# DVE's order beside the convolutions of a hybrid decoder layer: taps first, the weight remainder in two halves around the other work

## What is computed

```python
xn = rmsnorm(h, norm1_w[layer])
proj = xn @ w_in[layer]
q, k, v, z, xbc, dt_raw, ga_raw, gs_raw = _split(proj, IN_SPLITS)
attn = banded_sink_attention(q, k, v, attn_sinks[layer]) @ w_attn_o[layer]
xbc = jax.nn.silu(causal_dwconv(xbc, ssd_conv_w[layer], ssd_conv_b[layer]))
xs, bm, cm = _split(xbc, (D_INNER, BC_DIM, BC_DIM))
y = ssd_chunked(xs.reshape(Bsz, S, N_SSD_HEADS, SSD_HEAD_DIM), dt, a_log[layer], ...)
```

## The kernel before

| stage | DVE: unit, slot | PE: needs it at unit, slot |
|---|---|---|
| probabilities 5 | (9, 0) slot 0 | (9, 1) slot 0, L1321 |
| probs_t_masked 5 | (9, 1) slot 0 | (10, 0) slot 0, L1331 |
| probabilities 7 | (10, 1) slot 1 | (11, 0) slot 1, L1321 |
| probabilities 9 | (12, 1) slot 0 | (13, 0) slot 0, L1321 |
| probabilities 14 | (16, 0) slot 0 | (16, 1) slot 0, L1321 |
| decayed_cb 8 | (31, 0) slot 0 | (31, 1) slot 0, L1363 |

## Time and profile before

### The profile page before, as it was taken

How to read it: one execution, slowest core, us unless ns; L and a number is a source line. 1 busy time by engine, 2 the same in 40 slices (tenths; PEclk the granted TensorE clock), 3 DMA queues, 4 the chain that set the end, 5 groups by cost and what they waited for, 6 DMA issues and landing times.

```text
span 1028.8 us, 13393 instructions
## 1 busy us (share of the span) xinstructions
PE 1019.6 (99%) x5095; PEld 832.2 (81%) x5095; DVE 642.0 (62%) x909; ACT 457.5 (44%) x818; POOL 69.4 (7%) x112
## 2 busy tenths in 40 slices
PE   9999999999999999999999999999999999999997
PEld 8887777777788888888888888898888888888886
DVE  7636999794476685985754544666666676641323
ACT  6344555454555545765533222544444444331233
POOL 0000000000231120122220100000000000000000
PEclk9999999999999999999999999999999999999999
DMA  7622221225556424445362743223232223332322
GB/s 219 123 85 82 83 62 63 83 83 120 159 133 162 133 72 137 140 127 153 100 205 82 266 143 108 77 82 113 91 122 82 82 85 119 93 128 87 95 69 82
DMA packets 123498, 116.48 MB, mean 113 GB/s; under 512 B 21342, under 2 KB 111782, under 8 KB 123447
## 3 DMA queue, kind: packets, MB, share of 16 engines
q1 hardware_dynamic: 95509, 94.74, 29.9%
q10 hardware_dynamic: 25346, 12.59, 5.2%
q0 software_dynamic: 2592, 8.46, 2.2%
HBM read 109.41 MB, written 6.36 MB: 113 GB/s over the span
## 4 chain that ended last, share of the span: by engine, by line
PE 89%; DVE 8%; ACT 2%; issue 1%; DMA 0%; SPq 0%; ACTq 0%; DVEq 0%
PE banks L1259 27%; PE banks L1260 27%; PE banks L1261 27%; DVE conv_acc L1207 3%; PE banks L1363 1%; DVE w_lo L856 1%; PE banks L1356 1%; PE banks L1331 1%; PE banks L1351 1%; PE banks L1339 1%; DMA w_raw<-in_w_in 0%; ACT probs L614 0%; PE banks L1321 0%; PE banks L1311 0%; ACT w_hi L576 0%
## 5 line engine op out<-in xcount | busy, mean ns | idle before, releaser
L856 DVE TENSOR_TENSOR w_lo<-w_raw,w_hi 128x1024 fp32r<-128x1024 f32 (+1 forms) x166 | 198.3, 1234 | 123.7 <-ACT w_hi L576 122.4
L576 ACT ACTIVATE w_hi<-w_raw 128x1024 fp32r<-128x1024 f32 (+1 forms) x166 | 164.1, 1037 | 109.2 <-PE banks L1261 107.9
L1259 PE MATMUL banks<-xn_hi,w_hi 128*128 128x512 f32 x528 | 211.5, 401 | 0.0
L1260 PE MATMUL banks<-xn_lo,w_hi 128*128 128x512 f32 x528 | 206.1, 390 | 0.0
L1261 PE MATMUL banks<-xn_hi,w_lo 128*128 128x512 f32 x528 | 206.0, 390 | 0.0
L1259 PE MATMUL banks<-hn_hi,w_hi 128*128 128x512 f32 (+1 forms) x376 | 141.3, 376 | 0.0
L1260 PE MATMUL banks<-hn_lo,w_hi 128*128 128x512 f32 (+1 forms) x376 | 141.2, 375 | 0.0
L1261 PE MATMUL banks<-hn_hi,w_lo 128*128 128x512 f32 (+1 forms) x376 | 141.2, 375 | 0.0
L1259 PEld LDWEIGHTS banks<-xn_hi,w_hi 128*128 128x128 f32 x528 | 99.1, 188 | 28.2 <-issue 8.5
L1261 PEld LDWEIGHTS banks<-xn_hi,w_lo 128*128 128x128 f32 x528 | 99.1, 188 | 21.4
L1260 PEld LDWEIGHTS banks<-xn_lo,w_hi 128*128 128x128 f32 x528 | 99.3, 188 | 19.0
(11 more groups left out here) (221 smaller groups left out, 1429.8 us busy)
## 6 DMA issues: line engine op xcount, KB each, us to landing
w_raw<-in_w_in SPq DMA_DIRECT2D x29, 1024.0 KB, 5.4
w_raw<-in_w_up SPq DMA_DIRECT2D x22, 1024.0 KB, 5.0
decay<-acs_scratch ACTq DMA_DIRECT2D x16, 512.0 KB, 5.9
w_raw<-in_w_ssd_o SPq DMA_DIRECT2D x8, 1024.0 KB, 5.3
w_raw<-in_w_down SPq DMA_DIRECT2D x8, 1024.0 KB, 5.0
w_raw<-in_w_in SPq DMA_DIRECT2D x16, 256.0 KB, 4.5
w_raw<-in_w_attn_o SPq DMA_DIRECT2D x16, 256.0 KB, 4.7
decay_off<-acs_scratch ACTq DMA_DIRECT2D x32, 128.0 KB, 3.6
```

The costliest lines, as they stand in the source:

```text
L576: A.activation(whi[:, c % 2, lo_:hi_], raw[:, c % 2, lo_:hi_], ACT.Copy).then_inc(w_rounded, 1)
L856: V.tensor_tensor(wlo[:, c % 2, lo_:hi_], raw[:, c % 2, lo_:hi_], f32(whi[:, c % 2, lo_:hi_]), ALU.subtract).then_inc(w_split, 1)
L1259: T.matmul(out_, w[0], m[0], start=first, stop=False)
L1260: T.matmul(out_, w[0], m[1], start=False, stop=False)
```

## The change

In a chunk with a convolution, DVE no longer starts with the whole `split(c + 1)` and the rides of slot 0. For unit 0 its order is now: three taps, first half of `split(c + 1)`, rides of slots 0 and 1, second half, end of the silu (L1212, now L1218), rides of slot 2. For unit 1: three taps, rides of slots 0 and 1, end of the silu, rides of slot 2. In all other chunks nothing moves. No instruction is added or removed; only DVE's order differs.

```diff
-            def split(c, pairs=0):
+            def split(c, pairs=0, part=(0, 1)):
 
-                for k, (lo_, hi_) in enumerate(halves(c)):
+                for k in part:
+                    lo_, hi_ = halves(c)[k]
                     eng.wait_ge(w_rounded, 4 * pairs + (2 * c + k + 1))
...
-                elif 1 < c + 1 < len(CHUNKS) and c not in (AT[("out", 3)], AT[("up", 0)]):
+                elif 1 < c + 1 < len(CHUNKS) and c not in (AT[("out", 3)], AT[("up", 0)]) and kind not in ("bc", "xs"):
                     split(c + 1)
...
                 for u in range(2):
-                    rides(c, u, 0)
                     if kind not in ("bc", "xs"):
+                        rides(c, u, 0)
                         rides(c, u, 1)
...
+                        if u == 0:
+                            split(c + 1, part=(0,))
+                        rides(c, u, 0)
                         rides(c, u, 1)
+                        if u == 0:
+                            split(c + 1, part=(1,))
                         eng.wait_ge(c_tanh, k_conv + 1)
```

## The result

| | before | changed |
|---|---|---|
| median of the runs beside each other | 1030.29 us (1030.12 to 1030.65, 4 runs) | 1055.55 us (1054.08 to 1056.15, 4 runs) |
| ratio to before, 95% interval | 1 | 1.0243 (1.0225 to 1.026) |
| profiled execution, own time | 1030.5 us | 1054.08 us |
| its span | 1028.8 us | 1052.3 us |
| mean granted clock of PE in it | 0.999 | 0.992 |

Slower by 25.3 us, where 17.1 were forecast; the time lies above the range's 1054.

A forecast was written before the change was run, and what follows sets the result against it. PE, busy 1019.6 of 1028.8 us, was taken as the bound, so each new wait costs in full. Seven terms sum to 17.1 us on 1030.5, giving 1047.6, or 1047.4 for the median; range 1039 to 1054.

The forecast's parts named there:

- the clock: Rival: PE's clock falls at the two long waits, losing 1.65 us each, 3.3 in all: 1050.7 us; chance 0.15.
- Mechanism: DVE's taps wait for ACT's L772, so rides come late by 2.24 us, plus 1.13 for unit 0's half split.
- seven terms: PE's added waits at places from unit (9, 0) to chunks 31 to 33, 17.1 us in sum.
- term 7: Chunks 31 to 33: PE waits 2.5 us more for decayed_cb and 0.85 more for `x_dt`.
- Terms 1 to 6: Chunks 9 to 28: PE waits for late rides, lastly a late split: 3.95, 1.75, 1.3, 3.5, 2.2, 1.1 us.
- Covered at nothing (chunks 7 and 8): Probabilities and split still come over 1 us early in chunks 7 and 8, so no cost there.
- Signs in the profile: About 4 us PE idle before L1321, named releasers, DVE's idle before taps rising to some 15 us.
- the second rival: Lags don't add up over the long chains of steps; only 10.4 us are lost: 1040.7 us; chance 0.12.
- the third: Rival: faster by 2 us, as banks and tanh are free earlier and rides still make it: 1028.3 us; chance 0.03.
- No effect: Rival: DVE lags so far that L772 is always done before the taps: 1030.3 us; chance 0.04.

The follow-up runs named there:

- experiment 4: Changed kernel plus 16, 16 and 8 matmuls on constants in PE's waits for probabilities 5, 9 and 14: 1049.82 us.
- experiment 6: Kernel before with the new order in chunk 9 alone, plus 16 matmuls on constants in PE's wait for probabilities 5: 1035.7 us.
- experiment 5: Kernel before with the new order in chunk 9 alone, without filling matmuls: 1037.82 us.
- experiment 2: Changed kernel with the whole split back at the chunk's head, so only the rides of slot 0 moved behind the taps: 1043.47 us.
- experiment 1: Changed kernel with the rides of slot 0 back ahead of the taps, only the split's two halves staying behind them: 1041.09 us.
- experiment 3: Changed kernel plus 28, 28 and 14 matmuls on constants in PE's waits for probabilities 5, 9 and 14: 1053.76 us.
- experiment 7: Kernel before with only the split's second half moved behind the rides of slot 1 in convolution chunks: 1030.97 us, ratio 1.0005.

## Why the prediction was right or wrong

The step that failed is the clock, which the sum set at nothing after the long waits. The prediction had it as a rival with a chance of 0.15 and 3.3 us, and spoke against it that the waits "are hardly longer than the 3.3 us of that row, and it is one row". Experiments 4 and 6 show it as a cause: with PE busy in the waits, and nothing else changed, 5.6 and some 2 us went away. The rival's price was too small as well, though its upper bound of 6.6 held the measured 5.62. I counted two falls of 1.65; there were three, of 1.62, 2.41 and 1.59. The second lasted longer, some 6.8 us at the low level (182.4 to 189.2) where the first lasted 3.4. Transposes and scores stood behind both waits, so they don't tell the two apart. What differs in the rows is when the clock fell: 0.1 us after the first wait's end, but 1.7 us before the second's, and 1.1 before it in experiment 5, where it also stayed low for 6.8. What sets that moment no run here shows. The third fall I had not counted, since a wait of 2.1 is shorter than the 3.3 of my one row. The Trainium skill, "TensorE: Matmul & The Clock Gate", section "Why this matters for your kernels", which I had weighed and set aside, was right on the two long waits.

The other steps:

- **Mechanism: right.** The rides come late by the taps and the half split behind a wait for ACT's L772. All seven terms appeared at the place and with the releaser named. The largest loss of PE that no term named is 0.36 us at 465.36, for the second half of a split; the measured term 7 includes it.
- **Terms 1 to 6: right** within 0.15 us each. Laying out each engine's rows by hand with start-to-start prices held over a dozen steps.
- **Term 7: decayed_cb right (2.52), x_dt 10 undersized,** 1.58 for 0.85. Most of this is one DVE row that took 1.22 where it took 0.69 before; its rows are in the last section.
- **Covered at nothing (chunks 7 and 8): right.** Between the start-up and 123.7, PE waits for no ride and no split.
- **Signs in the profile: places right, DVE's idle wrong.** 29.0 us stood before the taps, for "some 15": I had counted idle time only in the units that hand something over late.
- **Rivals.** The lags do add up (18.16 against 17.1), so the second rival falls. Of the gain of the third there is no trace in the changed kernel, since no wait of PE was one for a bank. "No effect" falls with the first row on L1208.

What stays open: the other three timed runs of the changed kernel took 1055.3 to 1056.15 with a mean clock of 0.991, against 1054.08 and 0.992 for the profiled one. More or longer falls of the clock would fit, as in the two pairs of experiment 5; those runs have no trace, so this is argued. The lags and the clock give 17.1 + 1.1 + 5.6 = 23.8, and where the last 1.5 of the median's 25.3 went is not shown.

## What to carry to other kernels

Where one engine is the bound at 99%, an order that makes a helper engine wait first and serve later costs the whole delay, once for every result that had less slack than the delay; a piece of independent work (here one half of the split) must stay in front to fill the wait. Price a long wait of PE as the wait plus the slow matmuls behind it, 1.6 to 2.6 us here, and consider that a wait of 1.9 us can bring them too. Small waits left in a tuned order aren't simply to be had: removing two of them by hand gained 0.9 us in a trace and nothing that the timing could tell, and removing a third brought two others that took it back.

## What was not expected of the hardware

**A clock that falls well after a short wait.** The wait of 2.09 us ended at 239.45, and matmuls ran at full rate until they stretched, in the changed kernel's timeline of PE:

```profile
240.18 0.39 PE L1266 MATMUL banks<-xn_lo,w_hi 128*128 128x512 f32 x1
240.40 0.59 PE L1267 MATMUL banks<-xn_hi,w_lo 128*128 128x512 f32 x1
...
243.35 0.63 PE L1265 MATMUL banks<-xn_hi,w_hi 128*128 128x512 f32 x1
243.78 0.43 PE L1266 MATMUL banks<-xn_lo,w_hi 128*128 128x512 f32 x1
```

Starts are 0.43 us apart instead of 0.23, for 3.4 us, at half the clock and in the midst of dense work. The wait of 2.45 us at 443.08 brought nothing of the kind, nor did those of 1.5 to 1.7. In experiment 2 a wait of 1.88 us was followed by a fall and one of 2.20 us was not. So the length of a wait alone doesn't tell whether the clock falls.

**A DVE operation that stood behind one of POOL.** In the changed kernel around unit (32, 1), DVE and then POOL:

```profile
465.22 1.22 DVE L1218 SCALAR_TENSOR_TENSOR xs<-conv_tanh,conv_acc 128x512 f32<-128x512 f32 x1
...
464.91 0.98 POOL L558 TENSOR_TENSOR y_sq_pair<-y_off 128x256 f32<-128x256 f32 x1 [12.96 <-ACT y_off L672]
```

The same DVE operation takes 0.68 us everywhere else, and POOL's takes 0.74 where they don't meet, as in the kernel before (DVE's row at 441.05, done at 441.74, POOL's from 441.88). The pair met in the same way, at 1.22 and 0.98 (1.23 and 0.99 in the last), in experiments 1, 3, 4 and 7; in the others they didn't meet and took 0.68 and 0.74. The Trainium skill, "SBUF — State Buffer", section "Who interferes with whom", says that a DVE instruction with two inputs in SBUF and a GpSimd instruction that reads SBUF exclude each other, and the rows agree: L1218 reads `conv_tanh` and `conv_acc`. It delayed `x_dt` by 0.53 us and with it PE.
